# Decay tiles of a Mamba-2 scan: subtraction and clamp on ScalarE instead of VectorE

## What is computed

```python
acs = jnp.cumsum(dt * a.reshape(N_GROUPS, HEADS_PER_GROUP), axis=2)
causal = jnp.tril(jnp.ones((q, q), bool))[:, :, None, None]
seg = jnp.exp(jnp.where(causal, acs[:, :, :, None] - acs[:, :, None, :], -jnp.inf))
y_diag = jnp.einsum('bcqsgj,bcsgjp->bcqgjp', cb[..., None] * seg, xdt)
```

## Time and profile before

| | |
|---|---|
| median of three runs | 2355.98 us |
| the profiled execution | 2355.64 us, span 2353.9 us |
| PE busy | 2346.1 us, 100% |
| DVE busy | 1651.4 us, 70% (80 to 90% in the groups, which end near 900 us) |
| ACT busy | 1060.0 us, 45% |
| DMA | 453.95 MB, mean 193 GB/s |

### The profile page before, as it was taken

The page is one execution under the profiler, slowest core; times in us unless marked ns, Lnnn a source line. Parts: engine busy times, 40 slices in busy tenths (PEclk is TensorE's granted clock), DMA queues, the critical chain, the costliest instruction groups (busy, mean ns, idle before and its releaser), DMA issues.

```text
span 2353.9 us, 49580 instructions
## 1 busy us (share of the span) xinstructions
PE 2346.1 (100%) x19158; PEld 2299.7 (98%) x19158; DVE 1651.4 (70%) x3109; ACT 1060.0 (45%) x1583; POOL 109.2 (5%) x202
## 2 busy tenths in 40 slices
PE   9999999999999999999999999999999999999999
PEld 9999999999999999999999999999999999999998
DVE  7798988979888878798956555765555555544444
ACT  6453544535444445646633333554334333333333
POOL 1000000000000002101300000000000000000000
PEclk9999999999999999999999999999999999999999
DMA  7676767677676678566876765555555555555543
GB/s 215 199 225 206 242 189 216 212 214 235 189 225 212 206 239 241 152 194 177 250 204 193 205 211 182 182 171 161 162 169 160 170 162 159 174 197 168 169 159 117
DMA packets 546113, 453.95 MB, mean 193 GB/s; under 512 B 31184, under 2 KB 520112, under 8 KB 545408
## 3 DMA queue, kind: packets, MB, share of 16 engines
q1 hardware_dynamic: 525936, 406.23, 57.4%
q0 software_dynamic: 13392, 34.33, 4.5%
q10 hardware_dynamic: 6624, 11.18, 1.4%
HBM read 412.01 MB, written 38.81 MB: 192 GB/s over the span
## 4 chain that ended last, share of the span: by engine, by line
PE 97%; DVE 2%; issue 0%; ACT 0%; POOL 0%; DVEq 0%; ACTq 0%; POOLq 0%
PE acc L2097 30%; PE acc L2098 29%; PE acc L2099 29%; PE side L2084 1%; PE side L2183 1%; PE side L2235 1%; PE side L2107 0%; DVE cacc L1343 0%; PE side L2400 0%; PE side L2366 0%; PE side L2217 0%; PE acc L2579 0%; PE side L2579 0%; PE side L2577 0%; PE side L2578 0%
## 5 line engine op out<-in xcount | busy, mean ns | idle before, releaser
L1298 DVE TENSOR_TENSOR w_lo<-raw,w_hi 128x1024 fp32r<-128x1024 f32 (+2 forms) x692 | 830.2, 1207 | 513.2 <-ACT w_hi L793 507.7
L793 ACT ACTIVATE w_hi<-raw 128x1024 fp32r<-128x1024 f32 (+2 forms) x692 | 716.6, 1045 | 850.9 <-PE acc L2099 828.4
L2097 PE MATMUL acc<-h_hi,w_hi 128*128 128x288 f32 x3344 | 999.5, 299 | 0.0
L2099 PE MATMUL acc<-h_hi,w_lo 128*128 128x288 f32 x3344 | 986.0, 295 | 0.0
L2098 PE MATMUL acc<-h_lo,w_hi 128*128 128x288 f32 x3344 | 985.2, 295 | 0.0
L2097 PEld LDWEIGHTS acc<-h_hi,w_hi 128*128 128x128 f32 x3344 | 627.8, 188 | 15.5 <-issue 13.3
L2098 PEld LDWEIGHTS acc<-h_lo,w_hi 128*128 128x128 f32 x3344 | 627.4, 188 | 2.2 <-issue 2.2
L2099 PEld LDWEIGHTS acc<-h_hi,w_lo 128*128 128x128 f32 x3344 | 627.8, 188 | 0.0
L2097 PE MATMUL acc<-f_hi,w_hi 128*128 128x288 f32 x698 | 207.0, 296 | 0.0
L2099 PE MATMUL acc<-f_hi,w_lo 128*128 128x288 f32 x698 | 205.7, 295 | 0.0
L2098 PE MATMUL acc<-f_lo,w_hi 128*128 128x288 f32 x698 | 205.4, 294 | 0.0
(11 more groups left out here) (406 smaller groups left out, 2681.1 us busy)
## 6 DMA issues: line engine op xcount, KB each, us to landing
raw<-in_w_in_dram SPq DMA_DIRECT2D x512, 256.0 KB, 3.5
raw<-in_w_ffn_up_dram SPq DMA_DIRECT2D x352, 256.0 KB, 3.4
raw<-in_w_ffn_down_dram SPq DMA_DIRECT2D x160, 256.0 KB, 2.9
raw<-in_w_ssm_out_dram SPq DMA_DIRECT2D x128, 256.0 KB, 3.4
raw<-in_w_glu_dram SPq DMA_DIRECT2D x128, 256.0 KB, 3.7
h<-in_state_ssm_dram SPq DMA_DIRECT2D x32, 512.0 KB, 6.9
out_ssm_sample_dram<-h POOLq DMA_DIRECT2D x32, 512.0 KB, 3.8
raw<-in_w_out_dram SPq DMA_DIRECT2D x64, 256.0 KB, 3.2
```

The costliest lines, as they stand in the source:

```text
L793: copy = lambda out, in_, **k: nc.scalar.activation(out, in_, ACT.Copy, **k)
L1298: tt(w_lo[:, slot, 0:n], raw[:, slot, 0:n], w_hi[:, slot, 0:n].bitcast(F32), ALU.subtract).then_inc(lo_ready, 1)
L2097: mm(o_, wh, xh[:, kt, :], start=first and i == 0, stop=False)
L2099: done = mm(o_, wl, xh[:, kt, :], start=False, stop=last and i == n - 1)
```

## The change

DVE's `clamp` is gone. ACT's `seg_exp` now does, for each head, one Relu in place with scale -1 and the column of `gtv` as bias, which is the negative of the clamped difference, and then Exp with scale -1. The Relus count `seg_clamped` and ACT waits for its own last Relu before Exp. The calls move from steps 24, 25, 27 to 25, 26, 27 and stand behind `z_tanh` of the same step. ACT waits for the copy of `gtv` and for the DMA of `abc`, as DVE did. The copy of `gtv` stays on DVE at step 23. The arithmetic operations are the same in number, 24 of them and three Exp for each group.

```diff
@@ -849,10 +849,17 @@
             def seg_exp(c, g):
+                t0, n = TOK[c]
+                act.wait_ge(sem("heads_ready"), g + 1)
+                if c == 0:
+                    act.wait_ge(sem("acs_landed"), g * 64 + 64)
+                for j in range(HG):
+                    v = abc[0:n, j, t0:t0 + n]
+                    last = nc.scalar.activation(v, v, ACT.Relu, scale=-1.0, bias=gtv[0:n, ACS + c, j:j + 1])
+                last.then_inc(sem("seg_clamped"), 1)
                 act.wait_ge(sem("seg_clamped"), g * 3 + (c + 1))
-                t0, n = TOK[c]
                 v = abc[0:n, :, t0:t0 + n]
-                nc.scalar.activation(v, v, ACT.Exp).then_inc(sem("seg_exp"), 1)
+                nc.scalar.activation(v, v, ACT.Exp, scale=-1.0).then_inc(sem("seg_exp"), 1)
@@ -894,10 +901,10 @@
-                    if t in (24, 25, 27):
-                        seg_exp((24, 25, 27).index(t), n)
                     if t in (24, 25):
                         z_tanh(t - 24, n, chunk_at(g, 23), par)
+                    if t in (25, 26, 27):
+                        seg_exp(t - 25, n)
@@ -1368,16 +1375,6 @@
-            def clamp(c, g):
-
-                t0, n = TOK[c]
-                if c == 0:
-                    dve.wait_ge(sem("acs_landed"), g * 64 + 64)
-                for j in range(HG):
-                    v = abc[0:n, j, t0:t0 + n]
-                    last = ts(v, v, gtv[0:n, ACS + c, j:j + 1], 0.0, ALU.subtract, ALU.min)
-                last.then_inc(sem("seg_clamped"), 1)
@@ -1526,14 +1523,11 @@
-                    if t in (23, 24, 26):
-                        c = (23, 24, 26).index(t)
-                        if c == 0:
-                            if isinstance(n, int) and n == 0:
-                                dve.wait_ge(sem("dec_ready"), 1)
-                            dve.tensor_copy(gtv[:, :, :], tokv[:, :, ds(n * HG, HG)]).then_inc(sem("heads_ready"), 1)
-                            dve.wait_ge(sem("heads_ready"), n + 1)
-                        clamp(c, n)
+                    if t == 23:
+                        if isinstance(n, int) and n == 0:
+                            dve.wait_ge(sem("dec_ready"), 1)
+                        dve.tensor_copy(gtv[:, :, :], tokv[:, :, ds(n * HG, HG)]).then_inc(sem("heads_ready"), 1)
+                        dve.wait_ge(sem("heads_ready"), n + 1)
```

## The result

The changed kernel takes 2381.75 us (median of four runs, 2381.24 to 2382.39) against 2356.08 for the kernel before: 25.7 us more, a ratio of 1.011 with a 95% interval of 1.0092 to 1.0127. The forecast was 2375.0 in a range of 2365 to 2386. The profiled execution has a span of 2380.3 us, 26.4 over the span before.

What follows compares the result with a forecast made beforehand. PE was taken to bound the kernel (97% of the chain). Late chunk 1 starts, 16.1 us into groups 2 to 7, 2.9 into group 1 and 0 into group 0, add 19.0 to 2355.98: 2375.0 us, range 2365 to 2386.

Steps and rivals of the forecast that it cites:

- The bound and the place: PE bounds the kernel; only its waits count, and a new one comes at the z SiLU before chunk 1.
- The Relu: On ACT, priced from a row with one per-partition column: 0.385 us each, pitch 0.295, eight in 2.45 us.
- rival (b): Relu is not in the table Exp and Tanh share; six loads a boundary, 7.7 us, seven times: 2429 us; 2%.
- The walk on ACT: ACT's instructions from y_hi through steps 24 to 27: hi(0) 3.5 us late, so chunk 1 starts 2.7 us late.
- The cover of 0.84 us: Slack between z SiLUs' end and chunk 1: hi(0) may slip 0.84 us free; beyond it PE slips one for one.
- Into group 0: First boundary: z costs nothing; second large mask ends about 106.1, needed at 106.5; costed at nothing, at most 1 us.
- The sum of the late starts: Chunk 1 late at seven boundaries: 16.1 us into groups 2 to 7, 2.9 into group 1, 0 into group 0.
- rival (c): PE's clock halves over one chunk after each new wait: 2.6 us x 7 = 18 us, 2393 us; 5%.
- the prediction's own sign: What would show the forecast wrong in the new trace: here, a granted PE clock under 1.00.
- (d): The forecast's own mechanism holds, late z SiLUs delaying chunk 1: 2375.0 us likeliest, own error 2369 to 2382; 86%.
- its own terms (7 x 0.7 + 1): Forecast's own error: 0.7 us a boundary for pitches and order, plus up to 1 us at group 0.
- Rival (a): Not slower: hi(0) slips under 0.84 us, PE gets no new wait and gains 0.85 us at group 1: 2355.1; 7%.

Runs made afterwards that it cites:

- the kernel with the z work first: The changed kernel with z2 and z3 Tanh ahead of hi(0) on ACT and z SiLUs ahead of w_lo on DVE, step 0, groups 1 to 7: 2363.32 us.
- the eleven copies: The kernel before, clamps on DVE, plus eleven 128 x 128 copies to an unused tile on ACT ahead of hi(0), groups 1 to 7: 2384.18 us, ratio 1.0122.
- The spread kernel: The changed kernel with only the first eight Relus at step 25, the others at steps 2 and 4 of the next iteration: 2355.15 us, ratio 0.9997.

## Why the prediction was right, and where it fell short

**The bound and the place.** That only PE's waits count, and that the z SiLU ahead of chunk 1 is where a new one would appear, is borne out seven times in the list of waits and by the kernel with the z work first.

**The Relu.** Estimated 0.385 us each at a pitch of 0.295, eight in 2.45; the trace has 390 ns on average and eight in 2.44 to 2.45. The small ones: 0.31 and 1.85 estimated, 305 ns and 1.79 measured. The row with one column was the right one. No table load came with them, so rival (b) falls.

**The walk on ACT.** hi(0) was to slip by 3.5 us and slipped by 3.44; a cycle was to be 2.7 longer and is 2.66 longer where the clock is whole. Into group 1, chunk 0 was to start at about 168.8 and starts at 168.85; chunk 1 was to start at 177.75 and starts at 177.74, the same 2.9 late. The cover of 0.84 us is measured as 3.44 - 2.66 = 0.78; the eleven copies give nearly the same (hi(0) 3.73 late, the cycle 2.97 longer: 0.76), and 0.66 us did cost nothing. The waits as the list has them were to be 2.7 and 3.7 us and are 2.38 and 3.46, since the list counts them from the modelled end of the transposes. One slip had no effect: the lower pitch of the small Relus should be 0.227 - 0.09 = 0.137 us and not 0.12.

**Into group 0.** The second mask was to end at 106.1 and ended at 104.57 + 1.23 = 105.8. PE's matmuls of L2177 (the former L2183) start at 105.59 against 105.51, 0.08 us: nothing, as costed.

**What fell short.** The sum of the late starts, 19.0 us, measured 19.2. The rest of the span's 26.4, 7.1 us, is rival (c), which I had beside the forecast as an alternative with a chance of 5%, and so at nothing in the sum. By the prediction's own sign, a granted clock under 1.00 (it is 0.996 over the span), rival (c) came true. It was no alternative: it is a consequence of the forecast's own mechanism, and the right sum was (d) plus (c). That the total lies in the range all the same is luck: the upper half of the range was made for the error of the pitches, the bias and group 0, which came out right, and not for the clock. Worked out from its own terms (7 x 0.7 + 1), even that error ends at 2380.9 and not at 2382, below the 2381.75 measured. The size of (c) was off too, 7.1 and not 18, since the clock fell after four waits of seven and, three times, for a part of the chunk only. I had reasoned from the 0.9 us wait, after which the clock stays whole, to waits three times as long, about which it says nothing. The rule of the Trainium skill (TensorE: Matmul & The Clock Gate, Part 1), that an idle PE falls to half its clock, agrees with this trace for the longest wait: a pitch of 0.24 us in place of 0.133 after 3.46 us of idle time. For the others the trace shows more than the rule as I put it says: PE resumed at its full clock, which fell 1.2 to 1.45 us later at three of them and not at all at three.

**Rival (a)** was refuted for the changed kernel. The spread kernel, where the pile-up is gone, does what (a) says: 2355.15 against its 2355.1.

**What stays open.** Why the clock fell after the waits into groups 1, 3, 5 and 7 and not after those between, of equal length, and why the 3.5 us of copies led to falls at 2, 3, 5 and 6. No run here controls when a wait begins.

## What to carry to other kernels

An engine that is busy for under half of the span can be the one that sets a wait at one place, so find the steps where its work piles up and count the cover of what hangs behind it: here 0.84 us, under 3.4 us of added work, while the same work a few steps later cost nothing. Work taken off an engine that PE does not wait for is worth only the waits it ends, at most about 0.9 us here for 36 us of DVE time. Where new waits of PE as long as those of the changed kernel (2.4 to 3.5 us) are forecast, add the price of its clock to the sum as a term and not as a rival (here 7.1 us for seven waits, of which four were followed by a fall), and know that work which keeps PE busy through the wait gives that part back.

## What was not expected of the hardware

- PE's clock fell to 1.2 GHz after waits as short as 1.77 us in a kernel that is otherwise dense, and not after others of 2.4 to 2.9 us. Except after the 3.46 us it fell only when PE was at work again, 0.8 to 1.6 us into chunk 1. A fall cost 1.5 us three times (14 matmuls at 0.24 in place of 0.133 us), 2.6 us once.
- Useless matmuls made a kernel faster: 24 more transposes in each of seven waits, 6.9 us in all.
- Copies that each wait for the one before follow at about 0.34 us (eleven in 3.71), where the same shape's copies that do not wait follow at about 0.2 (four in 0.91, in the kernel before).
- The clock also fell, in some executions, in the last 50 us. In the kernel with the z work first the last stretches have 0.91 (2340 to 2350) and 0.78 (2350 to 2362). With two copies of 0.3 us added, it was 0.66 from 2340 to 2350, where the kernel before had 1.00. That profiled span was 2356.5 against 2353.9 before, with no wait in the groups that was not there before: 0.9 of the 2.6 us arose in the first 54 matmuls (9.06 us against 8.18), the other 1.7 lie behind chunk 1 of group 7. The kernel before has such executions as well (5 of 21 at 2357.55 to 2358.15 us with a mean clock of 0.998 or 0.999), but no trace of one. So about 2 us of a difference can come from this alone, and what sets it off is open.
